# Transfers of a phase issued in the phase before it, output weights in pieces, and stores awaited one phase later

## The reference

```python
for layer in range(DEPTH):
    if layer % 2 == 0:
        y, k, v, pst = even_mixer(rmsnorm(h_p, norm_g[layer]), pos_p, zeros_pool, sb_prompt, *wa)
        h_p = h_p + y
        ...
    else:
        y, C, n, m, cv = odd_mixer(rmsnorm(h_p, norm_g[layer]), zeros_conv, init, mlstm_prompt, *wc)
        h_p = h_p + y
        ...

def even_mixer(xn, ...):            # attention and a pooling mixer side by side
    ...
    mixed = jnp.concatenate([o_a * jax.nn.silu(g_a), o_b * jax.nn.silu(g_b)], axis=-1)
    return mixed @ w_out, ...

def odd_mixer(xn, conv_prefix, state, scan_fn, w_in, b_gate, conv_w, conv_b, w_q, w_k, w_v, skip, on_g, w_out):
    proj = xn @ w_in                 # x (2048), z (2048), gates (4 + 4)
    ...
    ca = jax.nn.silu(conv)
    q = jnp.einsum('bthd,hde->bhte', ca_h, w_q)
    k = jnp.einsum('bthd,hde->bhte', ca_h, w_k) * (DH_C ** -0.5)
    v = jnp.einsum('bthd,hde->bhte', xm.reshape(B, T, H_C, DH_C), w_v)
    h, C, n, m = scan_fn(state, q, k, v, logi, logf)      # 4 heads of 512
    out = (head_layernorm(h, on_g) + skip * ca) * jax.nn.silu(z)
    return out @ w_out, C, n, m, ...
```

## Time and profile before

| | us |
|---|---|
| median of 3 runs | 2444.93 |
| lowest, highest | 2442.22, 2451.13 |
| profiled execution | 2445.97 |
| its span, first to last instruction | 2444.2 |
| PE busy | 2116.6 (87% of the span) |
| DVE busy | 1073.5 (44%) |
| ACT busy | 650.8 (27%) |
| POOL busy | 94.4 (4%) |

### The profile page before, as it was taken

The page is one execution under the profiler, slowest core; times in us unless marked ns, Lnnn a source line. Parts: engine busy times, 40 slices in busy tenths (PEclk is TensorE's granted clock), DMA queues, the critical chain, the costliest instruction groups (busy, mean ns, idle before and its releaser), DMA issues. The chain is left out here.

```text
span 2444.2 us, 28078 instructions
## 1 busy us (share of the span) xinstructions
PE 2116.6 (87%) x10945; PEld 1546.2 (63%) x10945; DVE 1073.5 (44%) x1840; ACT 650.8 (27%) x1116; POOL 94.4 (4%) x149
## 2 busy tenths in 40 slices
PE   4979797969966579799999959999999999967998
PEld 2646464644433234499999949559569569535885
DVE  4060606061122212264444335675675675666442
ACT  3151515050012111133222233133123133114221
POOL 0000000000000000000000000110110110110000
PEclk8989898989988789899999979999999999988999
DMA  3010101015036331358658442452552551449561
GB/s 118 16 38 10 42 8 44 8 34 170 21 104 198 113 146 60 56 109 120 155 141 127 134 165 98 172 184 90 185 197 89 182 200 39 166 177 309 166 192 31
DMA packets 180241, 281.81 MB, mean 115 GB/s; under 512 B 15283, under 2 KB 114615, under 8 KB 179018
## 3 DMA queue, kind: packets, MB, share of 16 engines
q1 hardware_dynamic: 151013, 183.12, 27.7%
q0 software_dynamic: 24256, 88.82, 10.1%
q10 hardware_dynamic: 4864, 8.39, 1.1%
HBM read 185.17 MB, written 95.31 MB: 115 GB/s over the span
## 5 line engine op out<-in xcount | busy, mean ns | idle before, releaser
L1263 PE MATMUL pre_ps<-x_xh,pre_wh 128*128 128x358 f32 (+1 forms) x792 | 260.1, 328 | 13.2 <-DVE pre_wl L1385 13.2
L1264 PE MATMUL pre_ps<-norm_xl,pre_wh 128*128 128x358 f32 (+1 forms) x792 | 258.5, 326 | 0.0
L1265 PE MATMUL pre_ps<-x_xh,pre_wl 128*128 128x358 f32 (+1 forms) x792 | 258.4, 326 | 0.0
L389 PE MATMUL attn_ps<-x_xnT,attn_w 128*128 128x512 f32 (+1 forms) x576 | 193.7, 498 | 9.4 <-DMA attn_w<-in_w_in_a 7.5
L389 PEld LDWEIGHTS attn_ps<-x_xnT,attn_w 128*128 128x128 f32 x576 | 97.1, 194 | 105.9 <-issue 98.2
L1263 PEld LDWEIGHTS pre_ps<-x_xh,pre_wh 128*128 128x128 f32 x792 | 149.6, 189 | 14.6 <-DVE pre_wl L1385 13.7
L1264 PEld LDWEIGHTS pre_ps<-norm_xl,pre_wh 128*128 128x128 f32 x792 | 149.5, 189 | 0.0
L1265 PEld LDWEIGHTS pre_ps<-x_xh,pre_wl 128*128 128x128 f32 x792 | 149.4, 189 | 0.0
L649 PE MATMUL pool_ps<-x_xnT,pool_w 128*128 128x512 f32 (+1 forms) x384 | 131.2, 505 | 13.7 <-DMA pool_w<-in_w_in_a 8.7
L1028 PE MATMUL norm_yp<-norm_wo,even_mixT 128*128 128x512 f32 (+1 forms) x288 | 127.9, 603 | 15.3 <-DMA norm_wo<-in_w_out_a 15.3
L2308 PE MATMUL post_ps<-post_woh,post_oh 128*128 128x512 f32 (+1 forms) x288 | 114.8, 399 | 16.4 <-DVE post_ol L2402 15.4
(11 more groups left out here) (374 smaller groups left out, 3667.1 us busy)
## 6 DMA issues: line engine op xcount, KB each, us to landing
head_Cs<-in_state_C POOLq DMA_DIRECT2D x32, 1024.0 KB, 5.8
out_C_s<-head_Cs POOLq DMA_DIRECT2D x32, 1024.0 KB, 4.8
x_xnT<-in_cache_sb_k SPq DMA_DIRECT2D x64, 256.0 KB, 2.9
pre_w<-in_w_in_c SPq DMA_DIRECT2D x32, 512.0 KB, 9.9
x_dram<-low_low SPq DMA_DIRECT2D x16, 536.0 KB, 10.8
ca_dram<-low_low SPq DMA_DIRECT2D x16, 536.0 KB, 11.5
b_dram<-pre_bv SPq DMA_DIRECT2D x16, 536.0 KB, 7.6
a_dram<-low_low SPq DMA_DIRECT2D x16, 536.0 KB, 7.9
```

Source lines behind the costliest of these rows:

```text
L389: last = pe.matmul(ps[:, bank + c, 0:c1 - c0], w[:, u, k, :], xnT[:, k, c0:c1], start=(k == 0), stop=(k == KD - 1))
L1263: pe.matmul(out, wh[:, t % 2, k, :], xh[:, k, c0:c1], start=(k == 0), stop=False)
L1264: pe.matmul(out, wh[:, t % 2, k, :], xl[:, k, c0:c1], start=False, stop=False)
L1265: last = pe.matmul(out, wl[:, t % 2, k, :], xh[:, k, c0:c1], start=False, stop=(k == KD - 1))
```

## The change

Four handovers between phases are changed; the letters are used from here on.

**A**, start of the norm phase: `wo` comes in four pieces of 1 MB with a semaphore each, the first row tile of `x` behind the first piece. `project(0)` runs slice by slice with both halves inside, and waits for a piece at every second slice.

**B**, norm phase to input phase: POOL's memset, the two loads of gate weights and the loads of units 1 and 2 are moved into the norm phase, into a tile at the top of the on-chip memory that both phases leave free.

**C**, input phase to heads phase: at unit 25 SP waits until the gate rows and the first four blocks of x are stored, and loads head 0's `xr`, `w_v` and `w_k`. Small tiles are laid over others for the room.

**D**, heads phase to output phase: after its loop SP waits until head 3's projections are done and loads `a` and `b` of tile 0 and slices 0 to 5 of the output weights (3 MB), then, when head 3's first numerators are stored, the numerators of tile 0. POOL no longer waits for the landing of its stores; SP does so in the output phase, behind the load of tile 0's residual, and ACT does behind `normalise(0)`. Slices 6 to 15 come after that in five pieces of 1 MB. PE's order is now turn(0), `project_first()` (slice by slice with both halves, 96 matmuls), turn(1), project(1, first half), and the rest as before.

The diff, cut to its core (the rest renames tiles and passes them between the functions):

```diff
+def load_gates(nc, sp, d, w, w_in):
+    win = d["w_in_c"].rearrange("l (k p) c -> p (l k) c", p=P)
+    with nc.allow_non_contiguous_dma(reason="gate weights are a few words per row"):
+        for g in range(2):
+            c0 = 2 * INNER + HC * g
+            sp.dma_start(w[:, 0, :, S0 * g:S0 * g + HC], win[:, :, c0:c0 + HC]).then_inc(w_in[0], 16)
+def load_input(sp, d, w, w_in, u):
+    win = d["w_in_c"].rearrange("l (k p) c -> p (l k) c", p=P)
+    c0 = P * ((u - 1) // 2) + (0 if u % 2 else INNER)
+    sp.dma_start(w[:, u % WR], win[:, :, c0:c0 + P]).then_inc(w_in[u % WR], 16)
...
         @block.sync
         def _(sp):
-            sp.dma_start(wo[:, :, :], d["w_out_a"].rearrange("l (k p) c -> p (l k) c", p=P)).then_inc(wo_in, 16)
-            for i in range(XS):
+            for j in range(KD // 2):
+                sp.dma_start(wo[:, 2 * j:2 * j + 2, :], d["w_out_a"].rearrange("l (k p) c -> p (l k) c", p=P)[:, 2 * j:2 * j + 2, :]).then_inc(wo_in[j], 16)
+                if j == 0:
+                    sp.dma_start(x[:, 0, :], x_rows[0]).then_inc(x_in[0], 16)
+            for i in range(1, XS):
                 sp.dma_start(x[:, i, :], x_rows[i]).then_inc(x_in[i], 16)
             sp.dma_start(g[:, :], d["norm_g"][1:2, :].to_broadcast([P, D])).then_inc(g_in, 16)
+            sp.wait_ge(gate_zero, 1)
+            load_gates(nc, sp, d, w, w_in)
+            for u in range(1, WR):
+                load_input(sp, d, w, w_in, u)
...
             def project(i):
                 q, rows = i % 2, rows_of[i]
-                for half in range(2):
+                if i == 0:
+                    for k in range(KD):
+                        if k % 2 == 0:
+                            pe.wait_ge(wo_in[k // 2], 16)
+                        for half in range(2):
+                            last = pe.matmul(yp[0:rows, q, half, :], tok(mixT[:, k, :], i), wo[:, k, BANK * half:BANK * (half + 1)],
+                                             start=(k == 0), stop=(k == KD - 1))
+                for half in range(2 if i else 0):
                     for k in range(KD):
                         last = pe.matmul(yp[0:rows, q, half, :], tok(mixT[:, k, :], i), wo[:, k, BANK * half:BANK * (half + 1)],
                                          start=(k == 0), stop=(k == KD - 1))
...
-            pe.wait_ge(wo_in, 16)
             project(0)
...
         def _(pool):
+            pool.memset(w[:, 0], 0.0).then_inc(gate_zero, 1)
             for i in range(NT + 1):
...
-                sp.wait_ge(gate_zero, 1)
-                for g in range(2):
-                    c0 = 2 * INNER + HC * g
-                    sp.dma_start(w[:, 0, :, S0 * g:S0 * g + HC], win[:, :, c0:c0 + HC]).then_inc(w_in[0], 16)
                 for g in range(2):
...
-                load(1)
-                load(2)
                 for u in range(NU):
                     if u + WR < NU:
                         sp.wait_ge(wl_done, u + 1)
-                        load(u + WR)
+                        load_input(sp, d, w, w_in, u + WR)
...
+                    if u == 25:
+                        sp.wait_ge(gate_out, 80)
+                        sp.wait_ge(col_done, 1)
+                        for j in range(2):
+                            sp.wait_ge(x_out[j], 16 * KH // 2)
+                        sp.dma_start(xr[:, :, :], head_tokens(x_dram, 0)).then_inc(first[0], 16)
+                        sp.dma_start(hw[:, 0], square(d, "w_v", 0)).then_inc(first[1], 16)
+                        sp.dma_start(hw[:, 1], square(d, "w_k", 0)).then_inc(first[2], 16)
...
-        @block.gpsimd
-        def _(pool):
-            pool.memset(w[:, 0], 0.0).then_inc(gate_zero, 1)
...
             def load_x(e):
-                if e >= 1:
-                    sp.wait_ge(v_full, NV * e)
-                sp.dma_start(xr[:, :, :], head_rows(x_dram, e)).then_inc(x_in, 16)
+                sp.wait_ge(v_full, NV * e)
+                sp.dma_start(xr[:, :, :], head_tokens(x_dram, e)).then_inc(x_in, 16)
...
-            load_v(0)
-            load_x(0)
-            load_k(0)
+            def load_ahead():
+                num, a, bv, wo = ahead
+                src = d["w_out_c"].rearrange("l (k p) c -> p (l k) c", p=P)
+                sp.wait_ge(v_full, NV * HC)
+                sp.wait_ge(p_full, NJ * HC)
+                sp.dma_start(a[:, :, :], a_dram.rearrange("k p c -> p k c")[:, :, seq(0)]).then_inc(ahead_in[1], 16)
+                sp.dma_start(bv[:, :, :], b_dram.rearrange("k p c -> p k c")[:, :, seq(0)]).then_inc(ahead_in[2], 16)
+                sp.dma_start(wo[:, :, :], src[:, 0:WA_K, :]).then_inc(ahead_in[3], 16)
+                sp.wait_ge(num_out[0], 16 * (NT // 2) * (HC - 1) + 16)
+                sp.dma_start(num[:, :], num_dram[0]).then_inc(ahead_in[0], 16)
             for e in range(HC):
                 load_c(e)
                 load_rows(e)
...
                     load_x(e + 1)
                     load_k(e + 1)
                     load_v(e + 1)
+            load_ahead()
...
-            for j in range(2):
-                pool.wait_ge(num_out[j], 16 * (NT // 2) * HC)
-                pool.wait_ge(cs_out[j], 16 * (B // 2) * HC)
-            pool.wait_ge(c_out, 16 * HC)
-            pool.wait_ge(n_out, 16 * (KH + 1) * HC)
-            pool.wait_ge(snum_out, 16 * HC)
...
+        def heads_stored(eng):
+            for j in range(2):
+                eng.wait_ge(num_out[j], 16 * (NT // 2) * HC)
+                eng.wait_ge(cs_out[j], 16 * (B // 2) * HC)
+            eng.wait_ge(c_out, 16 * HC)
+            eng.wait_ge(n_out, 16 * (KH + 1) * HC)
+            eng.wait_ge(snum_out, 16 * HC)
...
                 j, (rows, c) = i % 2, rows_at(i)
                 if i >= 2:
                     sp.wait_ge(t_full, i - 1)
-                sp.dma_start(num[0:rows, j, :], num_dram[i, 0:rows]).then_inc(num_in[j], 16)
+                if i >= 1:
+                    sp.dma_start(num[j][0:rows, :], num_dram[i, 0:rows]).then_inc(num_in[j], 16)
                 if i >= 2:
                     sp.wait_ge(y_full, 2 * (i - 1))
-                sp.dma_start(a[:, j, :, 0:rows], a_dram.rearrange("k p c -> p k c")[:, :, c]).then_inc(a_in[j], 16)
-                sp.dma_start(bv[:, j, :, 0:rows], b_dram.rearrange("k p c -> p k c")[:, :, c]).then_inc(b_in[j], 16)
+                if i >= 1:
+                    sp.dma_start(a[j][:, :, 0:rows], a_dram.rearrange("k p c -> p k c")[:, :, c]).then_inc(a_in[j], 16)
+                    sp.dma_start(bv[j][:, :, 0:rows], b_dram.rearrange("k p c -> p k c")[:, :, c]).then_inc(b_in[j], 16)
                 if i >= 2:
                     sp.wait_ge(y_out[j], 16 * (i // 2))
                 src = h_dram[i] if i < NT else h_dram[i, S0:R8]
                 sp.dma_start(h[0:rows, j, :], src).then_inc(h_in[j], 16)
             load(0)
-            for k in range(4):
-                sp.dma_start(wo[:, 4 * k:4 * k + 4, :], src_w[:, 4 * k:4 * k + 4, :]).then_inc(wo_in[k], 16)
+            heads_stored(sp)
+            for j in range((KI - WA_K) // 2):
+                k = slice(WA_K + 2 * j, WA_K + 2 * j + 2)
+                sp.dma_start(wo_b[:, 2 * j:2 * j + 2, :], src_w[:, k, :]).then_inc(wo_in[j], 16)
             load(1)
...
                 for k in range(KI):
-                    if i == 0:
-                        pe.wait_ge(wol_done, k + 1)
                     if half == 0:
                         pe.wait_ge(ol_done, HC * i + k // KH + 1)
-                    high, low = oh[:, i % 2, k, 0:rows], ol[:, i % 2, k, 0:rows]
+                    high, low = oh[i % 2][:, k, 0:rows], ol[i % 2][:, k, 0:rows]
                     pe.matmul(out, high, woh[:, k, c], start=(k == 0), stop=False)
-                    pe.matmul(out, high, wol[:, k, c], start=False, stop=False)
+                    pe.matmul(out, high, wol_at(k)[:, c], start=False, stop=False)
                     last = pe.matmul(out, low, woh[:, k, c], start=False, stop=(k == KI - 1))
                 last.then_inc(y_full, 1)
+            def project_first():
+                for k in range(KI):
+                    pe.wait_ge(wol_done, k + 1)
+                    pe.wait_ge(ol_done, k // KH + 1)
+                    high, low = oh[0][:, k, :], ol[0][:, k, :]
+                    for half in range(2):
+                        c = slice(BANK * half, BANK * (half + 1))
+                        pe.matmul(ps[:, 4 + half, :], high, woh[:, k, c], start=(k == 0), stop=False)
+                        pe.matmul(ps[:, 4 + half, :], high, wol_at(k)[:, c], start=False, stop=False)
+                        last = pe.matmul(ps[:, 4 + half, :], low, woh[:, k, c], start=False, stop=(k == KI - 1))
+                        if k == KI - 1:
+                            last.then_inc(y_full, 1)
             turn(0)
-            for i in range(NT + 1):
+            project_first()
+            turn(1)
+            for i in range(1, NT + 1):
...
             def high_weights(k):
-                if k % 4 == 0:
```

(8 more changed lines are left out.)

138 lines of the change are left out of this document (85 added, 53 removed).

## The result

| | before | after |
|---|---|---|
| median of 4 runs each | 2447.3 us | 2422.86 us |
| lowest, highest | 2442.22, 2451.13 | 2417.96, 2426.97 |
| ratio, 95% interval | | 0.990 (0.988 to 0.992) |
| span of the profiled execution | 2444.2 us | 2423.1 us |
| PE busy | 2116.6 us | 2126.3 us |

The change wins 24.4 us by the medians and 21.1 us by the two traces. Forecast was a gain of 39.1, to 2406 us, with a range of 2399 to 2419. The direction was right, the size was not.

The account below looks back on a forecast made before the run. TensorE bounds the long stretches; time is lost at four phase handovers, where engines stand and the clock is at half. Gains 7.1+6.0+11.2+15.8-1.0 = 39.1 us give 2406 us, range 2399 to 2419.

Parts of the forecast that it names:

- so I take the first: Heads to output: POOL's drain takes a fixed 3.1 us even with stores in flight, so the release comes at 2187.1.
- The reading that turned out right: End of heads: POOL's drain waits until stores land and a little more; 5.6 us less gain, chance 0.31 with another reading.
- From T0 to the first matmul stays 6.47 us: Output phase: the first matmul follows the start of the output weights' split by 6.47 us, as before.
- T0: Output phase: when ScalarE starts to split the output weights; 2214.12 before, forecast 2192.8 at the first release.
- so what is won here reaches the end: Output phase: PE is busy without a gap from 2240 on, so the 15.8 us won by tile 1 stay won.
- The 1 us for the early loads beside head 3's states: Heads phase: the early numerators' load may delay a later state load by 2.6 us; priced at 1 us (0 to 3).
- the landing in the drain: End of heads, rival: POOL's drain waits for its stores; 5.6 or 8.6 us less, 2411.5 or 2414.5; chance 0.31.

Follow-up runs that it names:

- e1_again: The changed kernel run once more, unchanged: 2427.34 us median, ratio 0.991 to the kernel before.
- e8_best: The changed kernel plus early transposes of tile 1, head 3's last stores issued by SP, and two weight slices split early: 2408.35 us, ratio 0.985.
- e5_sp_stores: The changed kernel with head 3's last stores issued by SP instead of POOL, awaited in the output phase: 2416.38 us, ratio 0.987.

## Why the prediction was wrong

- **A**, 7.1 forecast, 9.0 measured, at the upper end of its range. PE waited for none of the later pieces: its 7.6 us of waiting for weights are the wait for the first. By the Trainium skill ("DMA: Bandwidth & Descriptors", section "Queues, rings and completion order") transfers of one issuing engine need not complete in order; no run here shows a piece that was late for it. The first 1 MB landed a little sooner than the 5.4 us of the earlier trace rows, and the clock's earlier rise was not in the sum.
- **B**, 6.0 forecast, 6.1 measured, less 0.8 for the clock. I had said that nothing changes there.
- **C**, 11.2 forecast, 11.3 measured.
- **D**, 15.8 forecast, 0.9 us of loss measured, which the spread of the stretch can't tell from nothing. This is the term that failed, in three steps:
  - *"so I take the first"*, the drain of a fixed 3.1 us. It lasts until POOL's own stores have landed, and took 11.6. The release came 1.3 us sooner and not 8.6: 7.3 us. Of the three rows of drains, the norm phase's fitted both readings, and the one that I read as a fixed cost stood behind waits that had already absorbed the landing. A drain behind such waits can't show whether it would wait by itself; on that question the row bore nothing, and I counted it. The reading that turned out right had 0.31 together with a worse one.
  - *"From T0 to the first matmul stays 6.47 us"*. It was 12.5: 6 us. In the trace of before, DVE's gating of tile 0 lay in the shadow of the wait for the weights (2205.18 to 2212.4, above). With the weights there, the gating was next in line on DVE, ahead of their low parts. The sum moved one wait and kept the length behind it, without asking what else had used the time. The kernel with the early split won 3.7 of the 6 us back by DVE's order alone.
  - *"so what is won here reaches the end"*. Up to tile 1 the rest of the sum held: from the first matmul to tile 1's it was 31.9 us, as forecast, and the gap and the clock behind it came as described (2.7 us where 2.4 were put). But every later tile takes 0.4 us more, 2.7 us in all, for a reason that the runs did not find.

  Together these are 7.3+6.0+2.7 = 16.0 us of the 16.7 between forecast and measurement.
- The 1 us for the early loads beside head 3's states did not show: PE's waits for the states' loads were 2.5 us over the whole phase and had been 2.3.

With A to D as measured the sum is 9.0+5.3+11.3-0.9 = 24.7 us, which is what the medians say (24.4, and 22.3 in e1_again). The traces' 21.1 has 4.5 us less for the heads phase, and 0.9 more for a start of the norm phase that came earlier. Head 0 alone accounts for the 4.5: up to the same matmul it took 98.7 us for 93.4, since A, B and C together let it begin at a time from which the clock stays down longer. My sum had assumed that a phase begun earlier takes as long as before, and had put nothing for this. The rivals: the landing in the drain was foreseen with 2411 to 2415; it was the right mechanism, but the gate in the way of the first matmul and the slower tiles put the time 8 to 11 us above even that. The range ended at 2419, since none of its cases had a longer way from T0 to the first matmul.

## What to carry to other kernels

When a wait is taken away, look in the trace at what else ran beneath it: the engine's own order decides what comes next, and here DVE's gating stood exactly where the weights' transfer had been. A semaphore wait ahead of a phase's end is not shown to be the cost while the drain behind it may wait for the same thing; here it paid to issue the last stores from the engine whose drain doesn't wait, and to await them one phase later (9.8 us less than awaiting them later alone; the other issuer alone brought 2.6). Compare parts by a stretch of the trace that holds the part and little else, since the clock elsewhere can move the whole by more than the part is worth.

## What the runs showed of the hardware

- POOL's drain waits for the landing of the transfers that POOL issued: 11.5 to 12.4 us in six traces with the last head's stores just issued, ending 1.5 us behind the last landing in the changed kernel; 6.6 to 7.5 us in six traces in which its last stores were one of 1 MB and one of 0.25 MB; 3.08 us, the same 3078 ns in eight traces of six kernels, behind semaphore waits for all landings.
- SP's drain does not: in e8_best and e5_sp_stores it took 0.12 us right behind the issue of SP's last store, and in e8_best the last of these stores landed 7.7 us behind the release.
- In the heads phase TensorE's clock falls to half several times, and how long it stays there in head 0 went with the time at which the phase began: 24 us in head 0 in all ten traces in which it began by 1421.6, 7 to 14 us in all ten in which it began later, two of them by a pure delay of 5.3 us. With the same waits of PE ahead of it (0.8 and 1.0 us), the clock fell 81.4 to 81.6 us behind head 0's first matmul in the former and 90 to 92 us behind it in the latter, and the same stretch of matmuls took 19.4 to 19.5 us or 12.6 to 13.4. The whole phase took 726 to 744 us for the same work. Why is open. Adding 5 us of idle time ahead of head 0 made neither of two kernels measurably slower.
